# Another order of the seven products of a full FFN block, with fewer combines on VectorE

## The reference, cut to what matters

```
def swiglu(h, w_in, w_out):
    u, v = jnp.split(h @ w_in, 2, axis=-1)
    return (jax.nn.silu(u) * v) @ w_out

x = x + 0.5 * swiglu(rmsnorm(x, norm_ffn1), ffn1_w_in, ffn1_w_out)      # D_FF = 2816
x = x + hybrid_mixer(rmsnorm(x, norm_mix), ...)
x = x + 0.5 * swiglu(rmsnorm(x, norm_ffn2), ffn2_w_in, ffn2_w_out)
```

## Time and profile before

| | us |
|---|---|
| median of 3 runs | 1142.19 |
| lowest, highest | 1141.85, 1143.57 |
| the profiled execution's own time | 1144.03 |
| its span, first to last instruction | 1142.2 |
| mean granted TensorE clock, of full speed | 0.997 |
| first FFN, block 1 to D2 | about 35 to 338 |
| mixer | about 338 to 760 |
| second FFN | about 760 to 1142 |

### The profile page before, as it was taken

How to read it: one execution, slowest core, us unless ns; L and a number is a source line. 1 busy time by engine, 2 the same in 40 slices (tenths; PEclk the granted TensorE clock), 3 DMA queues, 4 the chain that set the end, 5 groups by cost and what they waited for, 6 DMA issues and landing times.

```text
span 1142.2 us, 16722 instructions
## 1 busy us (share of the span) xinstructions
PE 1123.4 (98%) x6799; PEld 925.1 (81%) x6799; DVE 788.8 (69%) x1110; ACT 517.7 (45%) x757; POOL 137.0 (12%) x174
## 2 busy tenths in 40 slices
PE   8999999999999999999999999999999999999997
PEld 6778888888888987877778888888887888888885
DVE  7985888679955466566676344555795789459845
ACT  6642564245534233443445523356742565146533
POOL 1000000000010472346771000000000000000000
PEclk9999999999999999999999999999999999999999
DMA  8051326113514631413132232522052226204401
GB/s 305 24 203 37 111 74 221 37 43 106 184 47 122 153 84 43 96 54 82 45 83 50 75 101 80 181 90 101 10 184 74 74 74 221 74 8 141 147 1 74
DMA packets 111548, 111.78 MB, mean 98 GB/s; under 512 B 30896, under 2 KB 76384, under 8 KB 111472
## 3 DMA queue, kind: packets, MB, share of 16 engines
q1 hardware_dynamic: 106912, 104.97, 29.0%
q0 software_dynamic: 4400, 5.61, 1.8%
q10 hardware_dynamic: 160, 0.14, 0.0%
HBM read 105.71 MB, written 2.10 MB: 94 GB/s over the span
## 4 chain that ended last, share of the span: by engine, by line
PE 90%; DVE 7%; ACT 1%; issue 1%; DMA 0%; SPq 0%; DVEq 0%; ACTq 0%
PE ps L1994 11%; PE ps L1996 11%; PE ps L1995 11%; PE ps L1844 9%; PE ps L1845 8%; PE ps L1846 8%; PE ps L2010 6%; PE ps L2011 6%; PE ps L2012 6%; PE ps L1912 2%; PE ps L2128 2%; PE ps L2172 1%; PE ps L2201 1%; DVE w_lo L1500 1%; DVE probs L1458 1%
## 5 line engine op out<-in xcount | busy, mean ns | idle before, releaser
L1500 DVE TENSOR_TENSOR w_lo<-raw,w_hi 128x1024 fp32r<-128x1024 f32 (+1 forms) x124 | 142.0, 1185 | 65.0 <-ACT w_hi L1007 64.9
L1007 ACT ACTIVATE w_hi<-raw 128x1024 fp32r<-128x1024 f32 (+1 forms) x124 | 121.0, 1024 | 115.3 <-PE ps L2012 108.2
L2010 PE MATMUL ps<-w_hi,pu_hi 128*128 128x512 f32 x352 | 138.3, 393 | 0.1
L2012 PE MATMUL ps<-w_hi,pu_lo 128*128 128x512 f32 x352 | 137.1, 389 | 0.0
L2011 PE MATMUL ps<-w_lo,pu_hi 128*128 128x512 f32 x352 | 137.1, 389 | 0.0
L1994 PE MATMUL ps<-w_hi,xg_hi 128*128 128x512 f32 x320 | 125.3, 392 | 1.5 <-DVE square L1604 1.5
L1995 PE MATMUL ps<-w_lo,xg_hi 128*128 128x512 f32 x320 | 124.6, 389 | 0.0
L1996 PE MATMUL ps<-w_hi,xg_lo 128*128 128x512 f32 x320 | 124.5, 389 | 0.0
L1270 DVE TENSOR_TENSOR w_lo<-w_raw,w_hi 128x1024 fp32r<-128x1024 f32 (+4 forms) x42 | 75.3, 1793 | 54.6 <-ACT w_hi L890 54.6
L1844 PE MATMUL ps<-xg_hi,w_hi 128*128 128x512 f32 x272 | 108.5, 399 | 0.0
L1846 PE MATMUL ps<-xg_hi,w_lo 128*128 128x512 f32 x272 | 106.1, 390 | 0.0
(11 more groups left out here) (287 smaller groups left out, 2155.9 us busy)
## 6 DMA issues: line engine op xcount, KB each, us to landing
raw<-in_ffn_w_in SPq DMA_DIRECT2D x20, 1024.0 KB, 4.9
w_raw<-in_ffn_w_in SPq DMA_DIRECT2D x20, 1024.0 KB, 5.0
w_raw<-in_w_in SPq DMA_DIRECT2D x32, 512.0 KB, 4.3
raw<-in_ffn_w_out SPq DMA_DIRECT2D x14, 1024.0 KB, 5.9
w_raw<-in_ffn_w_out SPq DMA_DIRECT2D x6, 1024.0 KB, 4.9
w_raw<-in_w_in SPq DMA_DIRECT2D x24, 256.0 KB, 3.9
raw<-in_ffn_w_in SPq DMA_DIRECT2D x16, 256.0 KB, 5.7
w_raw<-in_w_out SPq DMA_DIRECT2D x8, 512.0 KB, 4.4
```

The costliest lines, as they stand in the source:

```text
L1007: nc.scalar.activation(w_hi[:, (BASE[i] + g) % 2, part], op_raw(g)[:, part], ACT.Copy).then_inc(up_sems["op_hi"], 1)
L1500: V.tensor_tensor(w_lo[:, sl, part], op_raw(g)[:, part], w_hi[:, sl, part].bitcast(F32), ALU.subtract).then_inc(up_sems["op_lo"], 1)
L2010: mm(bank, ph, wh, start=(k == 0 and start), stop=False)
L2012: last = mm(bank, pl, wh, start=False, stop=(stop and k == nk - 1))
```

## The change

The order of the seven products becomes A11, S3, A12, S2, S1, S4, A22 with the weight operands B11, B12 - B22, B21, T2, T1, B22, T4. Three banks per half are called x (0, 1), z (2, 3) and y (4, 5): the first product starts x, the second y, the third z, the fourth to sixth are added on in x and the seventh in y. ScalarE still copies three running sums out: x after the first product, y after the second, x after the fourth. VectorE makes three combines (v11, the new c22, v21) and two products with silu per half. ScalarE's negated copy goes; T2 is now (B12 - B22) - B11 and T1 is T2 + B22. Silu of one result reads PSUM (bank x) where it read SBUF, and of the other SBUF where it read PSUM.

```diff
-        OPERAND = (B11, B_DIFF, B21, B12, B22, B_MINUS, B21)
-        D_RAW = (3, 1, 2, 4)
+        OPERAND = (B11, B_DIFF, B21, B_T2, B12, B22, B21)
+        D_RAW = ((4, 2, 3, 1), (4, 2, 3, 1), (4, 2, 3, 4))
...
     pe_unit
-                    bank = up_bank("first" if o in (2, 6) else "second" if o == 4 else "chain", g, u)
+                    bank = up_bank("z" if o == 2 else "y" if o in (1, 6) else "x", g, u)
-                        goes_on = o in (1, 3, 5)
+                        goes_on = o > 2
...
     pe_bank_free
+            elif o == 5:
+                pe.wait_ge(*up(i, "c22", 2 * n + g + 1))
             else:
-                pe.wait_ge(*up(i, "v11", 2 * n + g + 1))
+                pe.wait_ge(*up(i, "chain_copied", 6 * n + {3: 0, 4: 4, 6: 2}[o] + g + 1))
```

VectorE's order in a full block (`dve_unit`):

```diff
-            dve_t1(dve, i, u)
+            dve_t2(dve, i, u)
             dve_op(dve, i, g0 + 2)
...
+            dve_t1(dve, i, u)
             dve_op(dve, i, g0 + 3)
-            dve_t2(dve, i, u)
...
             for g in range(2):
+                dve_v11(dve, i, u, g)
             dve_op(dve, i, g0 + 4)
             dve_t4(dve, i, u)
-            (w7 of both halves)
             dve_op(dve, i, g0 + 5)
-            (w5 of both halves, e1 of both halves)
+            for g in range(2):
+                dve_c22(dve, i, u, g)
             dve_op(dve, i, g0 + 6)
             if u % 2 == 0:
                 dve_diff(dve, i, u + 1)
-            (u12 and y of both halves)
             dve_op(dve, i, g0 + 7)
```

```diff
+        def dve_c22(dve, i, u, g):
+            n = u - 1
+            dve.wait_ge(*up(i, "product", 14 * n + 8 + g + 1))
+            dve.wait_ge(*up(i, "chain_copied", 6 * n + 2 + g + 1))
+            V.tensor_tensor(lane(u, g, 1), up_bank("x", g, u), lane(u, g, 1), ALU.add).then_inc(up_sems["c22"], 1)
```

```diff
     dve_plain
-            for o in (S1, S2, S4):
+            for o in (S1, S2, S4) if i else (S1,):
                 dve_sum(dve, i, o)
...
+            if i == 0:
+                dve_sum(dve, i, S2)
+                dve_sum(dve, i, S4)
     act_unit
             act_op(act, i, g0 + 1)
-            act_minus(act, i, u)
+            if u == 1 and i == 0:
+                for o in SUMS[1:]:
+                    act_sum(act, i, o)
```

```diff
     block.sync
             load_pair(sp, 0, 0, ffn1_w_in)
-            load_x(0, 0, 2, 2)
             load_pair(sp, 0, 1, ffn1_w_in)
     block.scalar
+            load_x(act, 0, 0, 2, 2)
             act.dma_start(vec_rows[0:KD, :], ...)
```

```diff
                     gd = first_op(*before_unit(n))
                     sp.wait_ge(*up(i, "op_lo", 2 * gd))
                     load_up(sp, i, n, B21, wi)
-                    sp.wait_ge(*up(i, "op_lo", 2 * (gd + 1)))
+                    sp.wait_ge(*up(i, "op_lo", 2 * (gd + 2)))
+                    load_up(sp, i, n, B11, wi)
+                    sp.wait_ge(*up(i, "op_lo", 2 * (gd + 3)))
                     load_up(sp, i, n, B12, wi)
-                    sp.wait_ge(*up(i, "op_lo", 2 * (gd + 2)))
+                    sp.wait_ge(*up(i, "op_lo", 2 * (gd + 4)))
                     load_up(sp, i, n, B22, wi)
-                    sp.wait_ge(*up(i, "op_lo", 2 * (gd + 3)))
-                    load_up(sp, i, n, B11, wi)
```

```diff
     pe_attend
                 for nn in (n, n + 1):
                     if nn < b - 1:
                         pe_values(pe, nn)
+                    if nn == n and n + 3 < b and ITEMS[n + 3][0] == "cmp":
+                        pe_scores(pe, n + 3, 1)
```

More of the change, by code:

```diff
@@ L312, in op_raw @@
                 return raw_of(n, OPERAND[g - g0])
-            return raws[D_RAW[g - g0]][:, 0:ktiles_of(2 * n + (g - g0) % 2) * T]
+            return raws[D_RAW[n][g - g0]][:, 0:ktiles_of(2 * n + (g - g0) % 2) * T]
         RAW_COUNT, raw_at = [0] * 5, {}
         for kind, n, g0 in SEGMENTS[1:]:
-            for b, r in ((B11, 2), (B12, 3), (B22, 1), (B21, 0)) if kind == "U" else enumerate(D_RAW):
+            for b, r in ((B11, 2), (B12, 3), (B22, 1), (B21, 0)) if kind == "U" else enumerate(D_RAW[n]):
                 RAW_COUNT[r] += 16
@@ L365, in build @@
         per_ffn = {"xs_ready": KD, "sum_ready": 4, "a_hi": 4, "a_lo": 4, "nat_psum": 0, "nat_ready": 0, "nat_squared": TT,
-                   "plain": 1 + TT, "silu_plain": TT, "minus": 5, "diff": 5, "t1_ready": 5, "t2_ready": 5, "t4_ready": 5,
-                   "op_hi": 2 * OPS, "op_lo": 2 * OPS, "product": 70, "down": 48, "chain_copied": 30, "v11": 10, "w7": 10,
-                   "w5": 10, "e1": 10, "u12": 10, "y": 10, "v21": 10, "silu12": 10, "silu22": 10, "prod1": 12, "prod2": 12,
+                   "plain": 1 + TT, "silu_plain": TT, "diff": 5, "t1_ready": 5, "t2_ready": 5, "t4_ready": 5,
+                   "op_hi": 2 * OPS, "op_lo": 2 * OPS, "product": 70, "down": 48, "chain_copied": 30, "v11": 10, "c22": 10, "v21": 10, "silu12": 10, "silu22": 10, "prod1": 12, "prod2": 12,
                    "transposed": 24, "p_hi": 24, "p_lo": 24, "added": 24}
@@ L603, in up_bank @@
         def up_bank(kind, g, u):
-            return ps[:, {"chain": 0, "first": 2, "second": 4}[kind] + g, 0:cols_of(u)]
+            return ps[:, {"x": 0, "z": 2, "y": 4}[kind] + g, 0:cols_of(u)]
         def prod_lane(u, half, g):
@@ L1076, in act_plain @@
             act_op(act, i, 2)
-            act_sum(act, i, S1)
             if i == 0:
@@ L1925, in pe_bank_free @@
                 else:
-                    pe.wait_ge(*up(i, "y", 2 * (n - 1) + g + 1))
-            elif o == 2:
-                if kind == "P":
-                    pe.wait_ge(*up(i, "prod2" if g else "prod1", 2))
-                else:
-                    pe.wait_ge(*up(i, "v21", 2 * (n - 1) + g + 1))
-            elif o == 4:
+                    pe.wait_ge(*up(i, "silu12", 2 * (n - 1) + g + 1))
+            elif o == 1:
                 if kind == "P":
@@ L2097, in pe_chunk, with pe_scores @@
                 last.then_inc(proj_psum, 1)
-        def pe_scores(pe, n):
+        def pe_scores(pe, n, part=0):
             it, b = ITEMS[n], 2 * (n % 2)
-            if n >= 2:
+            if n >= 2 and part == 0:
                 pe.wait_ge(pt_act, n - 1)
             if it[0] == "cmp":
-                for g in range(2):
+                for g in range(2 if part == 0 else 0):
                     mm(ps[:, b + g, :].rearrange("p (q h n) -> p q h n", q=TT, h=HPG), ident_b,
@@ L2107, in pe_scores @@
                        start=True, stop=False)
-                for qt in range(TT):
+                for qt in range(2 * part, 2 * part + 2):
                     for hh in range(HPG):
```

150 lines of the change are left out of this document (69 added, 81 removed).

## The result

The changed kernel takes 1148.83 us (median of six executions, 1146.93 to 1149.23) where the kernel before, on the same chip, takes 1142.22 (six, 1141.85 to 1143.57). The ratio, taken over all executions, is 1.0053, 95% interval 1.004 to 1.0066: slower by 0.53%, some 6.1 us; the two medians are 6.6 us apart. The forecast was 1142.3, with a range up to 1144.3.

What follows compares the result with a forecast made beforehand. The prediction took TensorE to bound the full blocks, with VectorE racing it in the first FFN's opening. Blocks 0, start 0 and scores +0.15 gave a median of 1142.3 us, range 1139.7 to 1144.3.

Steps and rivals of the forecast that it cites:

- The blocks: Ten full blocks: some 48 us of VectorE and 19 of ScalarE work removed under a never-stopping TensorE; cost 0.
- rival D: Full blocks: c22 comes 0.3 to 0.7 us late, delaying the sixth product; +3 to +7 us; 6%.
- The scores: Compressed scores: pe_values placed after 128 of 256 narrow matmuls shrinks the 2.38 us stall to about 1.7; net +0.15.
- Rival B: Compressed scores: instructions arrive during pe_values, so the split breaks the stall; -3.5 us, 1138.8; 9%.
- The +0.15: Compressed scores: last score 0.15 us later, 76 narrow matmuls left after the stall instead of 64; bounds +0.8 and -3.5.
- (b): First FFN's start: S2 and S4 sums deferred, some 2.5 us; TensorE's 1.5 wait goes, some 2.7 comes at the turn.
- (a): First FFN's start: first x transfer put first on ScalarE's queue; 0.9 us gained, at least 0, at most 1.08.
- the "0": First FFN's start: 2.4 us saved before the first full product becomes a wait at the turn; bounds -2.4 and +0.3.
- Rival C: First full block: clock falls once more behind the new 2.7 us wait; +1.7 us, 1144.0; 20%.
- a first full product near 33.2: Sign of the mechanism at the first FFN's start: first full product near 33.2, where it started at about 35.6.
- A: First FFN's start: the gain of 2.4 us is kept, 1139.9; 12%, about half of it counted as faster.

Runs made afterwards that it cites:

- both_back: Changed kernel with both start edits undone (x transfer back on SP's queue, S2 and S4 summed ahead of the plain unit); 1143.15 us, ratio 1.0001 to the kernel before.
- x_back: Changed kernel with the first x transfer back on SP's queue behind the first weights; 1144.92 us, ratio 1.002 to the kernel before.
- x_back_busy: Changed kernel with x back on SP's queue and ten unread matmuls in TensorE's wait at the turn; 1143.65 us, ratio 1.0016 to the kernel before.
- x_first_only: Kernel before with one edit, the first x transfer first on ScalarE's queue; 1145.21 us, ratio 1.0021.
- both_waits_busy: Changed kernel with ten unread matmuls at the turn and one more warm-up product before the first transposes; 1144.90 us, ratio 1.0022 to the kernel before.
- turn_late: x_back with the second half's turn one product later in the first FFN's first full block, ScalarE and VectorE queues reordered to match; 1141.68 us, ratio 0.999 to before.
- sums_back: Changed kernel with S2 and S4 summed ahead of the plain unit again, x still first on ScalarE's queue; 1145.96 us, ratio 1.0027 to the kernel before.

## Why the prediction was wrong

**The blocks: right.** Removed work lay under a TensorE that never stops, and VectorE's 45.8 us and ScalarE's 16.0 bought nothing. Those are a little under the forecast 48 to 54 and 19. c22, the difference after the first down product and the banks came where the steps put them; rival D had no part in it. both_back is the test of the whole part: 1.0001.

**The scores: right in kind.** The split's stall was put at 1.7 and measured 1.76, with 76 narrow matmuls behind it. Over all profiles with the split it is 1.07 to 1.78, over those without 2.08 to 2.68. From the first score to the transposes of the softmax it takes 11.9 to 12.6 us with the split and 12.0 to 12.6 without. Within either version this distance follows the stall one for one: it is the stall plus 10.85 with the split and plus 9.89 without. So the split shortens the stall by about the work that it puts ahead of it, and ends nothing sooner, which was the point of that step. Rival B is out. The +0.15 is too small to be told.

**(b): right in mechanism, its price hidden by (a).** The wait of 1.5 went, a wait of 2.5 came at the turn, and VectorE's chain from the second operand's residual to pu_lo is 10.15 us after (40.32 to 50.47) and 10.14 before. The start of it, in VectorE's timeline of the changed kernel, is the difference, the gated products, the two deferred sums (L1587) and the residual:

```profile
34.08 2.29 DVE L1514 TENSOR_TENSOR raw<-raw,w_raw 128x2048 f32<-128x2048 f32 x1
...
37.08 0.87 DVE L1617 SCALAR_TENSOR_TENSOR scratch<-ps,rstd_col,scratch 128x256 f32<-128x256 f32 x2
37.86 2.55 DVE L1587 TENSOR_TENSOR xs<-xs 128x1024 f32<-128x1024 f32 x2
40.32 2.36 DVE L1496 TENSOR_TENSOR w_lo<-raw,w_hi 128x1024 fp32r<-128x1024 f32 x2
```

The prediction had this chain start at 36.7, where it stands in the kernel before, because it took 0.9 off for the earlier x. In these steps the deferral by itself costs 0.9, and the 0.9 of (a) paid for it. With (a) out, the turn is 0.90 late in two kernels (48.29), whose second transposes stood 0.10 sooner than in the kernel before: 1.00. That a cancellation was behind the "0" was not said, and the upper bound of +0.3 for the sum didn't allow for losing either half. By the ratio (b) costs 1.3 us on the kernel before (interval 0.3 to 2.3), which this fits. Between both_back and x_back, which differ by (b) too, the ratios give 2.2; the turn explains 1.0 of them and the other 1.2 stay open, since x_back's profile shows the clock at 1.00 behind the turn.

**(a): the step that failed.** "They can gain that at most, and at least 0, since all transfers share the DMA engines. I take 0.9, near the upper end, since the row names x alone as the releaser." The row named x because x landed last. The constants had landed at about 4.9 (issued at 1.38, 3.5 to landing), and it was the edit that put them last. x itself came sooner, as the term had it: its two transfers were down at about 6.9 where they were at 7.45, 0.6 sooner for the 0.9. But the constants, issued at 2.44 behind it, took 6.3 and landed at about 8.7. The step looked at the transfer that moved and not at the two that it was moved ahead of, on a queue where the constants had stood ahead of any large transfer, nor at the 512 KB of weights that its leaving let out on SP's queue. Measured: first transposes 1.4 us later instead of 0.9 sooner. Without (a) the changed kernel loses 0.33% less (1.0053 to 1.002), some 3.8 us. The bound "at least 0" had left out that a transfer other than x could become the one that TensorE waits for.

**The clock: priced too low.** Rival C had 20%, 1.7 us and one place. The granted clock fell at two: behind the constants in every profile of the changed kernel (0.58 to 0.79 over 8 to 16), where the distance between the transposes grew by 1.2 to 2.3 us, and behind the turn in two profiles of three, 1.4 to 1.5 each. The argument against it, that the clock had stayed at 1.00 behind 2.38 us of waiting in the scores, was one execution's: in both_back, x_back_busy and x_first_only it fell 1 to 2 us behind the end of a stall of 1.75, 1.78 and 2.68. The places vary: both_waits_busy shows no fall in the scores at all, both_back has one from 452 to 456 (0.60), x_back one from 460 to 464 (0.57).

**The sum.** 2.63 for the late second transposes, in which the constants and the clock meet, and 1.00 for the deferral make 3.63; the turns of the two first profiles lie 3.65 apart. The medians are 6.6 apart, 3.0 more than the profiled executions: the changed kernel's profiled execution stands 1.2 below its median, and that of the kernel before 1.8 above its own. The 1.2 fit the fall behind the turn (1.4 to 1.5), which the first profile doesn't have and the other two do. The 1.8 may be the place of the fall in the scores. From the first score to the end of the span the profiles take 694.6 to 695.0 us where the clock fell ahead of the softmax's transposes (three) and 695.3 to 696.0 where it fell behind them (ten, the kernel before with 696.0). No second profile of the kernel before was taken to show that this is its 1.8.

The prediction named three things that would show it wrong: the turn's product clearly before 47.5, the "issue" wait gone, a combine in the table of waits. None came. What did was on the other side, a turn clearly after 47.5, and no bound had been set there. The list of what would show the mechanism did hold a sign, a first full product near 33.2, and that stood at 36.82. Two slips changed nothing: 192 - 126 is 66, and rival B with half of A is 15%, not 14.

## What to carry to other kernels

Before a transfer is moved to another queue, list what it is put ahead of there and what its leaving lets out where it stood; the first can land too late, the second can hold the transfer itself up, and the row that names it as the releaser says nothing of what will be last once the order is another. When a sum comes out at zero because two terms cancel, keep both as bounds and measure each by itself. Where an engine must wait for a slower one, look first for other work of its own to put there (turn_late gained 0.3% on x_back); a wait can cost more behind it than it lasts (sums_back: 1.7 us of wait, then 2.65 lost on the way to the second transposes, of which some 0.2 isn't the clock's).

## What the runs showed of the hardware

- **A wait inside busy stretches can cost more than its length.** In seven profiles with a wait of 1.4 to 2.8 us right ahead of the first transposes the granted clock fell behind it, and the way to the second ones took 1.1 to 2.7 us longer; in an eighth, with more warm-up before a wait of 1.6, it stayed at 1.00. The same kernel shows it in one execution and not in another (behind the turn: 1.00, 0.57, 0.69). The Trainium skill (TensorE: Matmul & The Clock Gate, What's actually happening) has the clock released by activity; the run that added matmuls nobody reads agrees: the clock stayed at 1.00 behind both filled waits.
- **A transfer's queue sets what it competes with.** x issued at 1.75 from SP's queue let the transposes start at 7.47; issued at 1.78 or 1.79 from ScalarE's, at 9.17, or 8.22 with the next weights held back. From 3 to 7 us, while x was under way, the DMA engines moved 302 GB/s in the kernel before and 301 in the one with x at 9.17, so about the same bytes landed, in another order. What the second queue costs by itself is not shown.
